# Feed-forward of a streaming encoder: two weight pairs to a group, 512-column steps, left-over sums through the activations

## What is computed

```python
def conv_ffn(h, buf, w_up, w_gate, conv_w, conv_b, w_down):
    L = h.shape[1]
    up = h @ w_up
    gate = h @ w_gate
    ext = jnp.concatenate([buf.astype(gate.dtype), gate], 1)
    act = jax.nn.gelu(causal_dwconv(ext, conv_w, L) + conv_b)
    return (act * up) @ w_down, ext[:, -(FFN_CONV - 1):]
...
        x = x + y
        y, fb = conv_ffn(rms_norm(x, p['norm_ffn'][l]), ffn_buf[l], p['w_up'][l], p['w_gate'][l],
                         p['ffn_conv_w'][l], p['ffn_conv_b'][l], p['w_down'][l])
        x = x + y
```

## Time and profile before

| what | value |
|---|---|
| runs, median | 2826.82 us |
| the profiled execution | 2826.28 us |
| its span | 2824.5 us |
| TensorE busy (matmuls) | 2805.3 us, 99% |
| TensorE weight loads busy | 2791.5 us, 99% |
| VectorE busy | 1555.3 us, 55% |
| ScalarE busy | 1032.5 us, 37% |
| read from memory | 412.92 MB, 148 GB/s over the span |

### The profile page before, as it was taken

One profiled execution on the slowest core, in us unless ns is written; L12 is line 12 of the kernel. 1 busy time (PEld: TensorE's weight loads), 2 busy tenths in 40 slices (PEclk: granted clock), 3 DMA queues, 4 the chain that ended last, 5 costly groups with the idle time before them and its releaser, 6 DMA issues.

```text
span 2824.5 us, 49617 instructions
## 1 busy us (share of the span) xinstructions
PE 2805.3 (99%) x19055; PEld 2791.5 (99%) x19055; DVE 1555.3 (55%) x2178; ACT 1032.5 (37%) x1135; POOL 123.6 (4%) x136
## 2 busy tenths in 40 slices
PE   9999999999999999999999999999999999999998
PEld 8999999999999999999999999999999999999998
DVE  7666645554355544555666666455554455535554
ACT  5443333333333333333444444443333333333333
POOL 0000021000000000002200000220000000000012
PEclk9999999999999999999999999999999999999999
DMA  6444344444444444444444444444444444444443
GB/s 237 145 145 137 129 149 149 151 148 151 151 149 144 155 150 149 142 155 149 144 146 151 136 143 142 154 147 151 148 150 149 149 149 149 149 149 149 149 149 114
DMA packets 120784, 420.26 MB, mean 149 GB/s; under 512 B 13688, under 2 KB 19840, under 8 KB 120576
## 3 DMA queue, kind: packets, MB, share of 16 engines
q1 hardware_dynamic: 120128, 418.45, 44.7%
q10 hardware_dynamic: 576, 0.66, 0.1%
HBM read 412.92 MB, written 6.14 MB: 148 GB/s over the span
## 4 chain that ended last, share of the span: by engine, by line
PE 98%; DVE 1%; DMA 0%; ACT 0%; issue 0%; DVEq 0%; ACTq 0%
PE gb L463 95%; PE ab L469 3%; PE ab L482 1%; DMA x<-in_x 0%; DVE w_lo L1097 0%; PE ab L663 0%; DVE work L1731 0%; DVE work L1225 0%; DVE rt L1727 0%; DVE work L1189 0%; ACT w_hi L785 0%; DVE a_lo L1104 0%; DVEq L140 0%; ACT work L862 0%; ACTq L850 0%
## 5 line engine op out<-in xcount | busy, mean ns | idle before, releaser
L1097 DVE TENSOR_TENSOR w_lo<-raw,w_hi 128x1024 fp32r<-128x1024 f32 x767 | 943.4, 1230 | 1175.5 <-ACT w_hi L785 1173.5
L785 ACT ACTIVATE w_hi<-raw 128x1024 fp32r<-128x1024 f32 x769 | 814.5, 1060 | 1653.8 <-PE gb L463 1651.4
L463 PE MATMUL gb<-a_hi,w_hi 128*128 128x320 f32 x4216 | 1311.1, 311 | 0.5 <-DVE w_lo L1097 0.3
L463 PE MATMUL gb<-a_hi,w_lo 128*128 128x320 f32 x4216 | 1302.8, 309 | 0.0
L463 PE MATMUL gb<-a_lo,w_hi 128*128 128x320 f32 x4216 | 1302.7, 309 | 0.0
L463 PEld LDWEIGHTS gb<-a_hi,w_hi 128*128 128x128 f32 x4216 | 791.6, 188 | 2.2 <-DVE w_lo L1097 0.6
L463 PEld LDWEIGHTS gb<-a_lo,w_hi 128*128 128x128 f32 x4216 | 791.6, 188 | 1.2
L463 PEld LDWEIGHTS gb<-a_hi,w_lo 128*128 128x128 f32 x4216 | 791.3, 188 | 0.0
L463 PE MATMUL gb<-b_hi,w_hi 128*128 128x320 f32 x1920 | 593.7, 309 | 0.0
L463 PE MATMUL gb<-b_hi,w_lo 128*128 128x320 f32 x1920 | 593.3, 309 | 0.0
L463 PE MATMUL gb<-b_lo,w_hi 128*128 128x320 f32 x1920 | 593.3, 309 | 0.0
(11 more groups left out here) (182 smaller groups left out, 804.6 us busy)
## 6 DMA issues: line engine op xcount, KB each, us to landing
raw<-in_weights SPq DMA_DIRECT2D x769, 512.0 KB, 3.3
out_y<-work SPq DMA_DIRECT2D x4, 640.0 KB, 3.0
out_c<-work SPq DMA_DIRECT2D x8, 257.0 KB, 5.6
x<-in_x SPq DMA_DIRECT2D x3, 640.0 KB, 7.8
work<-m_scratch SPq DMA_DIRECT2D x8, 192.0 KB, 4.9
work<-in_ret_tables SPq DMA_DIRECT2D x8, 160.0 KB, 3.3
work<-in_ml_state SPq DMA_DIRECT2D x8, 128.5 KB, 5.2
work<-in_w_pool SPq DMA_DIRECT2D x1, 1024.0 KB, 8.5
```

The source lines that it names most:

```text
L463: last = nc.tensor.matmul(bank(b, m), w[:, at:at + P], v[:, t:t + T], start=kg == k == n == 0, stop=kg == groups - 1 and k == UK - 1 and n ...
L785: nc.scalar.activation(w_hi[:, at:at + UW], raw[:, at:at + UW], ACT.Copy).then_inc(hi_ready, 1)
L1097: V.tensor_tensor(w_lo[:, at:at + UW], raw[:, at:at + UW], w_hi[:, at:at + UW].bitcast(F32), ALU.subtract).then_inc(lo_ready, 1)
```

## The change

It touches the feed-forward; elsewhere only the places of the high and low halves change: a and b now hold, for each tile, 320 high columns and behind them 320 low ones.

- Gate and up of two tiles (or two pairs of the down projection) are a group; they are worked at once, one k-group after the other. Two units, one of each pair, are a quad: 4 quads to a group, 3 in the last block. The units lie in memory in that order. All four banks of gb are open during a group.
- w_hi is multiplied with 512 columns in one matmul: the 320 high ones and the first 192 (WIDE_LO) low ones. w_lo is multiplied with the 320 high ones as before.
- The 128 low columns left over are summed the other way round (`left_of`): the 128 x 128 block of activations is the stationary operand and the four w_hi tiles of that k, 512 columns, stream. Its result in ab bank 1 has frames on partitions. VectorE turns 32 x 32 blocks (`turn_left`), ScalarE copies the 16 blocks to their places in two halves (`place_left`), VectorE adds them (`left_to_x`, or in `ffn_gate`).
- The left-over sum of a quad is made in the quad before, once its w_hi is there. In quads 1 and 3 the low weights come first, in quads 0 and 2 last.
- The group's banks are emptied at its end: `ffn_gate` for gate, `ffn_up` for up, or `add_wide_to_x` twice. The convolution comes after up is read.
- ScalarE's gelu and upper half, and the feed-in of the next mixer's tiles, move to other splits.

```diff
+WIDE_LO = 512 - T
...
-        a_hi, a_lo = sb("a_hi", KT * T, F32R), sb("a_lo", KT * T, F32R)
-        b_hi, b_lo = sb("b_hi", KT * T, F32R), sb("b_lo", KT * T, F32R)
+        a, b = sb("a", KT * 2 * T, F32R), sb("b", KT * 2 * T, F32R)
...
+        def high(ap, t):
+            return ap[:, bass.ds(t * 2 * T, T)]
+
+        def low(ap, t):
+            return ap[:, bass.ds(t * 2 * T + T, T)]
...
+            def left_of(u, q, quads, act):
+                for k in range(UK):
+                    t = (q * UK + k) * 2 * T + T + WIDE_LO
+                    w = w_hi[:, u.slot * UW:(u.slot + 2) * UW].rearrange("p (u k c) -> p u k c", u=2, k=UK)
+                    last = nc.tensor.matmul(left_bank, act[:, t:t + P], w[:, :, k, :], start=q == k == 0,
+                                            stop=q == quads - 1 and k == UK - 1)
+                return last
+            def wide_quad(u, q, quads, act, taken, group, apart=False, fresh=None):
+                final, low_first = q == quads - 1, q % 2 == 1
+                if q == 0:
+                    if fresh is not None:
+                        pe.wait_ge(fresh[0], fresh[1] + 2)
+                    pe.wait_ge(hi_ready, u.number(2))
+                    pe.wait_ge(left_turned, group)
+                    left_of(u, 0, quads, act)
+                def next_left():
+                    if final:
+                        return
+                    if fresh is not None:
+                        pe.wait_ge(fresh[0], fresh[1] + 2 * q + 4)
+                    pe.wait_ge(hi_ready, u.number(4))
+                    last = left_of(u.plus(2), q + 1, quads, act)
+                    if q + 1 == quads - 1:
+                        last.then_inc(left_summed, 1)
+                def high_weights(p):
+                    if q == 0:
+                        pe.wait_ge(pair_taken, taken + p)
+                    for m in range(UM):
+                        for k in range(UK):
+                            at, t = u.plus(p).slot * UW + (k * UM + m) * P, (q * UK + k) * 2 * T
+                            last = nc.tensor.matmul(gb[:, 2 * p + m, :], w_hi[:, at:at + P], act[:, t:t + 512],
+                                                    start=q == k == 0, stop=final and low_first and k == UK - 1)
+                    if low_first:
+                        last.then_inc(unit_used, 1)
+                def low_weights(p):
+                    pe.wait_ge(lo_ready, u.number(p + 1))
+                    for m in range(UM):
+                        for k in range(UK):
+                            at, t = u.plus(p).slot * UW + (k * UM + m) * P, (q * UK + k) * 2 * T
+                            last = nc.tensor.matmul(bank(p, m), w_lo[:, at:at + P], act[:, t:t + T],
+                                                    start=False, stop=final and not low_first and k == UK - 1)
+                    if not low_first:
+                        last.then_inc(unit_used, 1)
+                if apart and final:
+                    for p in range(2):
+                        high_weights(p)
+                        low_weights(p)
+                    return
+                if low_first:
+                    for p in range(2):
+                        low_weights(p)
+                    for p in range(2):
+                        high_weights(p)
+                    next_left()
+                    return
+                for p in range(2):
+                    high_weights(p)
+                next_left()
+                for p in range(2):
+                    low_weights(p)
...
+                        for q in range(4):
+                            wide_quad(Unit(u0 + 2 * q), q, 4, a, p0 - 1, group, fresh=(a_ready, a_base))
+                            if q == 1:
                                 norm(k_norm)
                         done = 1
...
+            def place_left(group, half):
+
+                act.wait_ge(left_turned, group + 1)
+                if half == 0:
+                    act.wait_ge(left_added, group)
+                for tokens in (2 * half, 2 * half + 1):
+                    for feats in range(4):
+                        last = nc.scalar.activation(left_t_blocks[feats * 32:(feats + 1) * 32, :, tokens, :],
+                                                    left_blocks[tokens * 32:(tokens + 1) * 32, :, feats, :], ACT.Copy)
+                last.then_inc(left_placed, 1)
...
+            def turn_left(group):
+
+                dve.wait_ge(left_summed, group + 1)
+                dve.wait_ge(left_placed, group * 2)
+                V.transpose(left, ab[:, 1, :]).then_inc(left_turned, 1)
+
+            def left_to_x(group, p):
+
+                dve.wait_ge(left_placed, group * 2 + 2)
+                at = x[:, bass.ds(p * 2 * T, 4 * T)].rearrange("p (m t) -> p m t", m=4)[:, :, WIDE_LO:T]
+                V.tensor_tensor(at, at, left_t.rearrange("p (m t) -> p m t", m=4), ALU.add).then_inc(left_added, 1)
+                dve.wait_ge(left_added, group + 1)
+
+            def add_wide_to_x(p, b, units, taken):
+
+                own()
+                used(units)
+                step.inc(V.tensor_tensor(two(tiles(x, p * 2)), banks(b), two(tiles(x, p * 2)), ALU.add))
+                own()
+                V.tensor_tensor(two(tiles(x, p * 2))[:, :, 0:WIDE_LO], lows_of(b),
+                                two(tiles(x, p * 2))[:, :, 0:WIDE_LO], ALU.add).then_inc(pair_taken, 1)
+                dve.wait_ge(pair_taken, taken)
...
-            def ffn_conv(layer, t, g, units, taken):
+            def ffn_gate(layer, t, units, group):
+
+                own()
+                ext = two(g_ext, GE)
                 s0 = 2 + SEQ + 2
                 V.tensor_scalar(ext[:, :, 2 + SEQ:s0],
                                 cols[:, bass.ds(t * 2 + COL[f"ffn_hist{layer}"], 4)]
                                 .rearrange("p (m t) -> p m t", m=2), 1.0, None, ALU.mult)
-                V.tensor_tensor(ext[:, :, 2:2 + SEQ], banks(0)[:, :, 0:SEQ], both(rt[:])[:, :, 0:SEQ], ALU.mult)
-                V.tensor_tensor(ext[:, :, s0:GE], banks(0)[:, :, SEQ:T], both(rt[:])[:, :, SEQ:T], ALU.mult)\
+                used(units)
+                r = both(rt[:])
+                V.tensor_tensor(two(low_gate)[:, :, 0:WIDE_LO], lows_of(0), r[:, :, 0:WIDE_LO], ALU.mult)
+                V.tensor_tensor(ext[:, :, 2:2 + SEQ], banks(0)[:, :, 0:SEQ], r[:, :, 0:SEQ], ALU.mult)
+                V.tensor_tensor(ext[:, :, s0:GE], banks(0)[:, :, SEQ:T], r[:, :, SEQ:T], ALU.mult)\
                     .then_inc(pair_taken, 1)
-                dve.wait_ge(pair_taken, taken)
+                dve.wait_ge(left_placed, group * 2 + 2)
+                V.tensor_tensor(low_both.rearrange("p (m t) -> p m t", m=4)[:, :, WIDE_LO:T],
+                                left_t.rearrange("p (m t) -> p m t", m=4),
+                                rt[:, WIDE_LO:T].unsqueeze(1).to_broadcast([P, 4, P]), ALU.mult)\
+                    .then_inc(left_added, 1)
+
+            def ffn_conv(layer, t, g):
+
+                dve.wait_ge(gate_scaled, g + 1)
+                ext, conv = two(g_ext, GE), two(g_conv, GW)
...
-            def ffn_up(g, units, taken):
+            def ffn_up(units, taken):
 
                 used(units)
-                V.tensor_tensor(two(up), banks(1), both(rt[:]), ALU.mult).then_inc(pair_taken, 1)
+                r, ext, s0 = both(rt[:]), two(g_ext, GE), 2 + SEQ + 2
+                V.tensor_tensor(two(low_up)[:, :, 0:WIDE_LO], lows_of(1), r[:, :, 0:WIDE_LO], ALU.mult)
+                V.tensor_tensor(two(up), banks(1), r, ALU.mult).then_inc(pair_taken, 1)
                 dve.wait_ge(pair_taken, taken)
+                lo = two(low_gate)
+                V.tensor_tensor(ext[:, :, 2:2 + SEQ], ext[:, :, 2:2 + SEQ], lo[:, :, 0:SEQ], ALU.add)
+                V.tensor_tensor(ext[:, :, s0:GE], ext[:, :, s0:GE], lo[:, :, SEQ:T], ALU.add).then_inc(gate_scaled, 1)
+                step.inc(V.tensor_tensor(up, up, low_up, ALU.add))
+
+            def ffn_product(g):
                 dve.wait_ge(gelu_ready, g + 1)
+                own()
                 act_ = two(g_act, GW)
...
-            weights[at:at + n] = np.stack([gate, up], 1).reshape(n, P, UW)
+            weights[at:at + n] = np.stack([gate, up], 2).reshape(n, P, UW)
             at += n
             n = KT // UM * (k // UK)
-            weights[at:at + n] = units_of(a["w_down"][layer][rows])
+            weights[at:at + n] = units_of(a["w_down"][layer][rows]).reshape(4, 2, k // UK, P, UW)\
+                .transpose(0, 2, 1, 3, 4).reshape(n, P, UW)
```

More of the change, by code:

```diff
@@ L558, in first_unit @@
                     for m in range(UM):
-                        at, t = (k * UM + m) * P, k * T
-                        for n, (w, v) in enumerate(((w_hi, a_hi), (w_hi, a_lo), (w_lo, a_hi))):
-                            last = nc.tensor.matmul(bank(0, m), w[:, at:at + P], v[:, t:t + T],
+                        at, hi, lo = (k * UM + m) * P, high(a, k), low(a, k)
```

(47 more changed lines are left out.)

315 lines of the change are left out of this document (181 added, 134 removed).

## The result

The changed kernel takes 2857.41 us (median of 4 runs, 2857.07 to 2857.97), the kernel before 2826.88 us beside it (median of 4, 2825.56 to 2827.31): a ratio of 1.0109, 95% interval 1.0091 to 1.0126. The forecast was 2793 us with a range of 2745 to 2836. The change is slower by 30 us, and the prediction was wrong in sign and range.

A forecast was written before the change was run, and what follows sets the result against it. TensorE's work, and new waits of TensorE, were taken to bound the kernel. From 2826.3 us, -42.2 for matmuls saved, +3 and +6 for bank waits and +1 at the end gave 2794, forecast as 2793 us; range 2745 to 2836.

The forecast's parts named there:

- What bounds the kernel: Whole kernel: TensorE is busy 99% of the span; only its work and new waits of it can move the end.
- Price of 512 columns: Feed-forward wide matmuls: 226.7 ns each, with 13.3 ns paid once per matmul; 264 quads save 0.160 us each, -42.2 us.
- Rival (a): TensorE's weight loads are the limit, so 512 columns cost 0.216 us; result 2748 us, chance 0.15.
- rival (b): Single-pass float32 matmuls cost 1.1 times the stream per column, so little is saved; 2828 to 2834 us, chance 0.25.
- The left-over chain: Transpose and 16 ScalarE copies at 0.20 us take 5.4 us, ready 2.9 us before the group's end; priced at nothing.
- Its sum is complete at E - 8.3 us: The left-over sum is complete 8.3 us before E, the end of an up/gate group's last matmul.
- Evacuation: VectorE emptying four banks at group end: waits of +3 us in 44 gate and up groups, +6 us in eight three-quad groups.
- The end, +1: Kernel's very end: the last two tiles of x are added in two steps, with a second addition; +1 us.
- Rival (c): Slow copies (0.46 us) or transpose place left-overs after E + 1; 68 groups wait, about +120 us, 2910 us, chance 0.10.
- a third of a us more in 68 groups: Upper end of the forecast's own range, 2785 to 2812 us: a third of a us more waiting per group.

The follow-up runs named there:

- run 1: Changed kernel with the 16 left-over copies a group replaced by two straight copies (blocks not put in their places): 2803.24 us, ratio 0.9916 to the kernel before.
- Run 2: Changed kernel with ten of the 16 left-over copies a group, the other six blocks left out: 2814.07 us, ratio 0.9958 to the kernel before.
- run 9: run 6 and run 7 together, plus the left-over product behind the emptying of up's banks on VectorE: 2793.25 us, ratio 0.9883 to the kernel before.
- run 6: Changed kernel with the last block's down projection of each layer back to 320-column matmuls without left-over sums: 2826.61 us, ratio 0.9999 to the kernel before.
- run 7: run 3 plus, in groups of four quads, ScalarE's second half of copies behind the split of the next group's second unit: 2843.1 us, ratio 1.0057.
- run 3: Changed kernel with the left-over addition to x behind the bank additions in down groups of four quads: 2839.49 us, ratio 1.0045 to the kernel before.
- run 10: run 9 with ScalarE's copies back at the change's place, ahead of the split of the next group's second unit: 2808.01 us, ratio 0.9935.

## Why the prediction was wrong

- *What bounds the kernel*: right. What TensorE does and waits for is the whole difference.
- *Price of 512 columns*, the step on which "the whole case hangs": right, 0.227 and 0.1467 us, and -42.2 us with it. The 13.3 ns are paid per matmul. Rival (a), the load as limit at 2748 us, and rival (b), per column at 2828 to 2834, both fall. The Trainium skill ("TensorE: Matmul & The Clock Gate", Back-to-back issue gap) gives an isolated warm matmul 2.5 ns beyond its columns; in this stream of matmuls with a load each, both shapes have 13.3. The Trainium skill ("Perfetto Trace Analysis", Identifying the Most-Contended Engine) takes the loads' busy share, with the share of peak flops, as the measure of how near TensorE is to its limit, and I had read the 99% as a point for (a); the loads fell to 89% and a wide matmul still took 13.3 ns over its stream.
- *The left-over chain, priced at nothing*: this is the step that failed. With 0.8 us of copies a group (run 1) the change is 54 us shorter. The size was off: I took 0.19 to 0.20 us from copy to copy and named 0.36 as the far bound; it is 0.32, 5.1 us for 16, as these small copies do not overlap by the 0.1 us that large ones do. Run 2 shows the forecast's price: 2814 us, faster by 0.4%. But the right size would not have saved the forecast: in its own sum 0.2 + 0.6 + 0.2 + 5.1 + 0.95 + 0.2 = 7.3 us is still inside the 8.3 us, so its own test would have passed again. The reasoning failed: I asked only whether the left-overs are ready before the group ends. They are, by 1.2 us in the down group shown. I did not ask what is queued behind the copies on ScalarE (the next group's splits) and behind the wait for them on VectorE (the bank additions). Those positions matter as much as the length: with the positions of the change and short copies (run 1) the groups of four quads wait 11.6 us, with all 16 copies and the positions of run 9 they wait 3.8, for 39.5 with the change.
- *"Its sum is complete at E - 8.3 us"*: true for four quads. With three it is one quad of high and low weights, 16 x 0.2267 + 16 x 0.1467 = 6.0 us before the end, and the 7.2 us of transpose, copies and the split between (744.0 to 751.2 in the down group shown) no longer fit. I priced 8 groups at 6 us that cost 23.
- *Evacuation*: down groups of four quads were left out of the sum (18.7 us; 2.5 with cheap copies). Gate and up: 3 forecast (0.06 us a group), 9.1 in runs 1 and 2, 20.8 with the change; so this term was too small by three times even without the copies. Run 9, with the left-over product behind up's reads, has next to nothing of it. Three quads: 6 forecast, 4.1 in run 1.
- *The end, +1*: 7.2. There all 16 copies lie on the path (5.11 us, up to 2834.15), ahead of the additions and of GpSimd's squares; with 0.8 us of copies it is 2.5 (run 1), without left-over sums 0.8 (run 6).
- *The mixer's start*, not in the sum: 5.9 us. TensorE waits 3.33 us for the last x additions, and the stretch at the lower clock behind it costs 1.8 more (72 matmuls of 320 columns in 12.32 us and not 10.56). It is 0.7 us in run 6.
- *Rival (c)* came nearest, but it is not what happened. It wanted copies of 0.46 us and left-overs placed after E + 1; here they were placed before E, and TensorE waited all the same, 0.92 us a group in the mean (62.5 / 68), at copies of 0.32 us. Its turning point of 0.62 us a group is sound (42 / 68), its copies of about 0.4 us are not.
- *Two sums that do not close*, without weight for what came: a third of a us more in 68 groups is 23 us, so the range's upper end would be 2816 and not 2812; and rival (b) takes 10 us of waits in one case and 8 in the other, which with 10 gives 2836.

## What to carry to other kernels

A helper chain that is "ready in time" for its own reader can still be late for all that is queued behind it. For every instruction that a change puts on a queue, list the next two on that queue and who waits for them, in each variant of the loop (here four and three quads) and at the end. When a reordering only moves a wait, look for the second one that receives it before undoing the first: here one move alone cost 4 us (run 7 against run 3) and was worth 15 once the other was made (run 9 against run 10). The version with both, and with the last block's down projection as before, is 1.2% faster than the kernel before.

## What the runs showed of the hardware

- A ScalarE copy of 32 x 128 float32 is recorded with 0.308 us and repeats every 0.32 us, so nothing of it overlaps with the next. The splits of 128 x 1024 do overlap: 1.06 us each, three in 2.96. A copy of 128 x 256, eight times the elements of the small one, takes 0.41 us (run 1). Sixteen pieces take 5.1 us for as many elements as two pieces move in 0.8.
- Single-pass float32 matmuls pay 13.3 ns beyond columns / 2.4 GHz at 320 and at 512 columns alike (steps of 0.1467 and 0.2267 us).
- VectorE's transpose of 128 x 512 from a PSUM bank takes 0.717 us, beside 0.68 for a product on the same number of columns.
- A wait of 2.15 us on a TensorE that was otherwise full was followed by 4 us at a granted clock of 0.57 in the mean; it cost 1.7 us more (5.50 for 3.79) after the wait was over. Three of six such waits did this, three did not.
